# Squares added on VectorE before TensorE sums them over the partitions

## What is computed

```python
def rms_norm(x, g):
    x32 = x.astype(jnp.float32)
    y = x32 * lax.rsqrt(jnp.mean(x32 * x32, axis=-1, keepdims=True) + EPS) * g.astype(jnp.float32)
    return y.astype(x.dtype)

for i in range(DEPTH):                                    # DEPTH = 2
    h = rms_norm(x, ln_mix_g[i])
    x = x + mixer_block(h, ...)      # proj = h @ w_in; q = rms_norm(q_lat, q_norm_g) @ w_uq; kv = rms_norm(kv_lat, ...) @ w_ukv
    h = rms_norm(x, ln_ffn_g[i])
    x = x + hier_moe(h, ...)
    h = rms_norm(x, ln_ple_g[i])
    x = x + jax.nn.sigmoid(h @ w_ple_gate[i]) * (p[i] @ w_ple[i])
return rms_norm(x, final_norm_g)
```

## Time and profile before

| | us |
|---|---|
| median of 3 runs | 1233.9 |
| the runs | 1229.99 to 1234.84 |
| the profiled execution | 1233.92 |
| its span, first to last instruction | 1232.1 |
| TensorE busy | 1135.8 (92%) |
| VectorE busy | 633.6 (51%) |
| ScalarE busy | 355.8 (29%) |
| GpSimd busy | 135.4 (11%) |

### The profile page before, as it was taken

The page is one execution under the profiler, slowest core; times in us unless marked ns, Lnnn a source line. Parts: engine busy times, 40 slices in busy tenths (PEclk is TensorE's granted clock), DMA queues, the critical chain, the costliest instruction groups (busy, mean ns, idle before and its releaser), DMA issues.

```text
span 1232.1 us, 22073 instructions
## 1 busy us (share of the span) xinstructions
PE 1135.8 (92%) x8320; PEld 901.5 (73%) x8320; DVE 633.6 (51%) x1325; ACT 355.8 (29%) x591; POOL 135.4 (11%) x169
## 2 busy tenths in 40 slices
PE   5998889999899999997889979999998999999976
PEld 5987879998765555554879769899986555555576
DVE  4575878655543333334446749775446333333344
ACT  4343443233331111113244344423334111111142
POOL 0110320011000000000102022101101000000001
PEclk9999989999999999998979989999998999999978
DMA  6535876447269999996325369654544999999911
GB/s 173 144 91 151 305 238 186 140 143 216 104 268 418 416 418 418 418 417 195 104 76 155 97 196 344 184 155 137 155 143 176 391 417 418 418 417 418 374 56 65
DMA packets 202708, 300.54 MB, mean 244 GB/s; under 512 B 13969, under 2 KB 166513, under 8 KB 186225
## 3 DMA queue, kind: packets, MB, share of 16 engines
q1 hardware_dynamic: 202608, 299.28, 68.6%
HBM read 298.21 MB, written 1.05 MB: 243 GB/s over the span
## 4 chain that ended last, share of the span: by engine, by line
PE 79%; DVE 8%; DMA 6%; ACT 2%; issue 2%; SPq 2%; POOL 0%; DVEq 0%; POOLq 0%; ACTq 0%
PE ps L688 77%; DMA gu_ring<-in_w_exp_up_dram 4%; PE ps L691 2%; DMA ring<-in_w_in_dram 2%; DVE wsplit L1592 2%; ACT wsplit L1137 1%; SPq L555 1%; SPq L551 1%; DVE work L1696 1%; DVE work L1668 1%; DVE work L1618 0%; DVE h_pair L1601 0%; DVE h_pair L1872 0%; DMA work<-in_x_dram 0%; DVE h_pair L1996 0%
## 5 line engine op out<-in xcount | busy, mean ns | idle before, releaser
L688 PE MATMUL ps<-h_pair,wsplit 128*128 128x256 f32 x3264 | 432.9, 295 | 40.0 <-DVE h_pair L1601 12.2
L688 PEld LDWEIGHTS ps<-h_pair,wsplit 128*128 128x128 f32 x3264 | 418.2, 201 | 50.8 <-issue 33.9
L1592 DVE TENSOR_TENSOR wsplit<-ring,wsplit 128x1024 fp32r<-128x1024 f32 x136 | 168.2, 1239 | 105.8 <-ACT wsplit L1137 95.7
L1137 ACT ACTIVATE wsplit<-ring 128x1024 fp32r<-128x1024 f32 x136 | 141.9, 1056 | 226.5 <-PE ps L688 155.6
L688 PE MATMUL ps<-gu_ring,hT 128*64 128x256 f32 x1280 | 153.7, 383 | 2.4 <-DMA gu_ring<-in_w_exp_up_dram 2.4
L688 PEld LDWEIGHTS ps<-gu_ring,hT 128*64 128x64 f32 x1280 | 88.2, 137 | 65.8 <-issue 20.1
L1696 DVE SCALAR_TENSOR_TENSOR work<-work,convT 128x256 f32<-128x256 f32 x240 | 100.9, 493 | 0.0
L1339 ACT ACTIVATE prow<-ps 128x128 f32<-128x128 f32 x64 | 17.7, 277 | 278.3 <-PE ps L688 278.3
L1959 DVE TENSOR_TENSOR hT_r<-ps,hT_r 128x512 fp32r<-128x512 f32 x64 | 44.3, 692 | 94.0 <-ACT hT_r L1137 94.0
L688 PE MATMUL ps<-work,ring 128*128 128x256 f32 x384 | 88.2, 386 | 0.0
L1945 DVE TENSOR_TENSOR prow<-prow,ps 128x128 f32<-128x128 f32 x64 | 18.4, 288 | 133.8 <-ACT prow L1339 133.8
(11 more groups left out here) (203 smaller groups left out, 1048.7 us busy)
## 6 DMA issues: line engine op xcount, KB each, us to landing
ring<-in_w_in_dram SPq DMA_DIRECT2D x104, 512.0 KB, 4.4
gu_ring<-in_w_exp_gate_dram SPq DMA_DIRECT2D x40, 1024.0 KB, 14.9
gu_ring<-in_w_exp_up_dram SPq DMA_DIRECT2D x40, 1024.0 KB, 17.2
down_ring<-in_w_exp_down_dram SPq DMA_DIRECT2D x40, 1024.0 KB, 19.3
lent_down<-in_w_exp_down_dram SPq DMA_DIRECT2D x24, 1024.0 KB, 19.8
ring<-in_w_exp_gate_dram SPq DMA_DIRECT2D x12, 1024.0 KB, 14.9
ring<-in_w_exp_up_dram SPq DMA_DIRECT2D x12, 1024.0 KB, 17.2
lent_gate_up<-in_w_exp_gate_dram SPq DMA_DIRECT2D x12, 1024.0 KB, 15.7
```

Source lines behind the costliest of these rows:

```text
L688: return nc.tensor.matmul(o, lhsT, rhs, start=first, stop=last)
L1137: return nc.scalar.activation(o, i, ACT.Copy)
L1592: TT(tile_split[:, m, 1, :, :], tile_of(name, m), tile_split[:, m, 0, :, :].bitcast(F32), ALU.subtract).then_inc(tile_low, 1)
```

## The change

VectorE adds the chunks of squares before TensorE sums over the partitions. The new function `add_squares` adds the second, third and fourth pair of chunks to the first pair (128x512 each, in place), and then the second chunk of that pair to the first (128x256). TensorE's `stat` is given that one chunk: 2 matmuls instead of 16 or 12. This is done for x at the start of a layer and at the end of the program, for the queries (two pairs and the halves) and for the embedding. The sums of keys and values and of the layer norm stay as they are. `sq_added` is a new semaphore; each addition waits for ScalarE's pair of squares and for the addition before it, and TensorE's sum waits for the last one.

```diff
+            def add_squares(name, sq, pairs):
+
+                done = SQUARES_ADDED.index(name)
+                for i in range(1, pairs):
+                    dve.wait_ge(sq_ready, after(SQUARES, f"{name}{i}"))
+                    if i > 1:
+                        dve.wait_ge(sq_added, done + i - 1)
+                    TT(sq[:, 0:2, :], sq[:, 0:2, :], sq[:, 2 * i:2 * i + 2, :], ALU.add).then_inc(sq_added, 1)
+                dve.wait_ge(sq_added, done + pairs - 1)
+                TT(sq[:, 0, :], sq[:, 0, :], sq[:, 1, :], ALU.add).then_inc(sq_added, 1)
...
                 project_split("kv", "mix")
-                stat("mix", [sq_x[:, c, :] for c in range(DC)], sq_events("mix", DC))
+                stat("mix", [sq_x[:, 0, :]], [(sq_added, all_added("mix"))])
...
                 project_split("gg0")
-                stat("q", [sq_q[:, c, :] for c in range(6)], sq_events("q", 6))
+                stat("q", [sq_q[:, 0, :]], [(sq_added, all_added("q"))])
...
                 project_split("pg0", "ple")
-                stat("ple", [sq_p[:, c, :] for c in range(DC)], sq_events("ple", DC))
+                stat("ple", [sq_p[:, 0, :]], [(sq_added, all_added("ple"))])
...
             begin(pe, DEPTH + 1)
-            stat("mix", [sq_x[:, c, :] for c in range(DC)], sq_events("mix", DC))
+            stat("mix", [sq_x[:, 0, :]], [(sq_added, all_added("mix"))])
...
                 low_tiles(l, "kv")
 
+                add_squares("mix", sq_x, 4)
                 mean("mix", D)
...
                 evacuates(TT(kr[NOPE:QK, 1, :], bank("rotk")[NOPE:QK, 0:S], sinT[NOPE:QK, :], ALU.mult), "rotk")
+                add_squares("q", sq_q, 3)
                 scale_out("gg0", two(glu_t[0][:, 0, :]))
...
                 low_pair(3)
+                add_squares("ple", sq_p, 4)
                 low_tile(l, "pg1", 0)
...
             begin(dve, DEPTH + 1)
+            add_squares("mix", sq_x, 4)
             mean("mix", D)
```

More of the change, by code:

```diff
@@ L127, with all_added @@
 POWS = ["mix", "kv", "q", "lnv", "ffn", "ple"]
+SQUARES_ADDED = ["mix"] * 4 + ["q"] * 3 + ["ple"] * 4
 SQUARES = ([f"mix{i}" for i in range(4)] + ["kv", "q0", "q1", "q2", "lnv"]
            + [f"ple{i}" for i in range(4)])
+def all_added(name):
+    return len(SQUARES_ADDED) - SQUARES_ADDED[::-1].index(name)
 def after(events, name):
@@ L340, in program @@
         sq_ready = lsem("sq_ready")
+        sq_added = lsem("sq_added")
         tile_high = lsem("tile_high")
@@ L720, in bcast @@
                 last.then_inc(bcast_ready, 1)
-            def sq_events(name, n):
-                return [(sq_ready, after(SQUARES, f"{name}{c // 2}")) for c in range(n)]
             with pe.Fori(0, DEPTH) as l:
```

## The result

| | before | after |
|---|---|---|
| median | 1232.8 (4 runs) | 1220.0 (4 runs) |
| the runs | 1229.99 to 1234.84 | 1217.69 to 1220.91 |
| the profiled execution | 1233.92 | 1220.91 |
| its span | 1232.1 | 1219.1 |

The ratio is 0.9894 with a 95% interval of 0.9869 to 0.9918: the kernel became 12.8 us faster. The forecast was 1207, with a range of 1202 to 1217, so the gain came out at half of what it said: 26.7 us were expected, and 13.0 separate the two profiled executions.

A forecast was written before the change was run, and what follows sets the result against it. The prediction took TensorE to bound the kernel (79% of the span). Matmuls 16.6, clock 9.0 and end 2.7, less 1.6 for a new wait, gave 26.7 us off 1233.9: 1207 us, range 1202 to 1217.

The forecast's parts named there:

- The matmuls removed: Shorter TensorE sums for x, queries and embedding save 3.1, 2.2 and 3.0 us a layer, 16.6 us in two.
- The clock behind the six sums: Behind the sums for x, queries and embedding the clock no longer falls to half: 9.0 us in two layers.
- Rival 1: The clock's falls belong to the stretch, not to the long sums, and stay: 1216 us, 12%.
- The additions: VectorE's additions for x and embedding end before TensorE asks: cost 0; four with handings-on take 2.7 us.
- Rival 3: Additions come late, TensorE waits at all seven sums and restarts at low clock: slower, 1248 us, 3%.
- The new wait: At the spread of the queries' norm TensorE waits 0.8 us for VectorE's diagonal, twice: 1.6 us lost.
- The end: The program's last sum, not hidden and at half clock, gets shorter though it waits for the additions: 2.7 us gained.
- Weights arrive for later stages by semaphores of the stages before: In later stages weight transfers start earlier along with the stages before, so nothing catches up on the gain.
- Rival 2: In the mixer a weight transfer hides the gain of the queries' sum and clock, 3.6 us a layer: 1214 us, 8%.

The follow-up runs named there:

- e10: The changed kernel with TensorE's common branch first and each one-column matmul on the added squares issued 4 times, 8 in a sum: 1212.1 us.
- e11: The changed kernel with TensorE's common branch first and one-column matmuls repeated to sums of 16 and 12, as before the change: 1232.4 us.
- e4: The changed kernel, additions kept, each one-column matmul on the added squares issued 8 times (6 for the queries): 1237.1 us.
- e7: The changed kernel with TensorE's two branches exchanged, so that it tests for the common case first: 1205.6 us.
- e9: The kernel before with TensorE's two branches exchanged, so that it tests for the common case first: 1229.4 us.
- e1: The changed kernel with 100 executed semaphore increments ahead of TensorE's first wait: 1212.0 us.
- e5: The changed kernel with 100 instructions in TensorE's branch for crowded experts, which is never executed: 1210.1 us.
- e2: The kernel before with 156 executed semaphore increments at TensorE's start: 1262.0 us.
- e3: The changed kernel with SyncE's 3 MB for the fifth expert asked for only after the first expert's first product: 1222.0 us.
- e6: The kernel before with 156 instructions in TensorE's branch for crowded experts, which is never executed: 1245.0 us.
- e12: The changed kernel with 200 instructions in TensorE's branch for crowded experts, which is never executed: 1212.2 us.

## Why the prediction was wrong, point by point

- **The matmuls removed, 16.6 us.** Right: 3.20, 2.24 and 3.12 us in layer 0 (forecast 3.1, 2.2, 3.0). The group of one-column matmuls has 108 records, as said.
- **The clock behind the six sums, 9.0 us.** Right in all six places: the key projection takes 3.51 (said: 3.5), gv0 6.0 without its wait (5.9), the first half of pg1 2.94 (3.0). e10 against e11 confirms the cause, and the size (1.6 a fall, against 9.0 / 6 = 1.5) as well as medians that vary by 4 us can. The Trainium skill's rule weighed there, by which a drop comes from an idle gap, doesn't fit these falls: in e4 and e11 they are back with no gap in TensorE's work just ahead of them. Rival 1 fell.
- **The additions, 0 in the layers.** Right. VectorE's timeline of the changed kernel at x, at the queries and at the end:

```profile
22.32 2.28 DVE L1569 TENSOR_TENSOR work<-work 128x512 f32<-128x512 f32 x3
24.64 0.42 DVE L1571 TENSOR_TENSOR work<-work 128x256 f32<-128x256 f32 x1
...
52.25 1.83 DVE L1569 TENSOR_TENSOR work<-work 128x512 f32<-128x512 f32 x2
54.12 0.42 DVE L1571 TENSOR_TENSOR work<-work 128x256 f32<-128x256 f32 x1
...
1207.98 2.28 DVE L1569 TENSOR_TENSOR work<-work 128x512 f32<-128x512 f32 x3 [1.96 <-ACT work L1147]
```

  Those at x end at 25.06, 0.8 us ahead of TensorE's sum, those of the embedding at 585.91 against 588.50. They take the forecast 2.7 us. Rival 3 wanted 1.8 an addition; only the queries' first ones are slowed, the two taking 1.83 beside GpSimd's work.
- **The new wait, 1.6 us.** 0.78 us twice, for `diag L1589`. The mechanism and the range (0.45 to 1.25) were right; that the middle taken in it fits to the tenth is luck.
- **The end, 2.7 us.** Right: the last sum starts 3.97 us behind the first square and is over 0.88 later, 4.85 in all. In the kernel before the transposes follow 7.53 us behind the first square (1217.32 and 1224.85), 2.7 more.
- **"Weights arrive for later stages by semaphores of the stages before, so their transfers start earlier with them and nothing catches up on the gain."** This step failed. The weights did start earlier, by 5.4 us (346.37 to 340.95); TensorE's waits for the experts' weights are not longer (2.3 us in all instead of 2.4). But the sum treated the removed instructions as time only and not as places in the program, and so put what else the change does to the experts' stage at nothing. Those 96 moved the end of a block to 12 instructions behind a branch target, next to a burst of 3 MB, at 6.5 to 7.3 us a layer (some 1.5 of it, in layer 0, may be a low clock that stands there without the stop too). No part of the profile of before shows this stop; only the wait of 1.6 us for "issue" at the branch, with 6 in total, hinted that fetching was on the path here. Rival 2, a transfer that takes part of the gain, was nearest in kind, but put it on the weights' side and in the mixer, and gave it 3.6 a layer.

What remains between the 26.7 forecast and the 23.8 of e7 against e9 is within what these runs vary (e7's own runs span 8 us), and the comparisons don't settle it: e1, with its padding taken off, stands 27.2 us below the kernel before, and e5 21.2.

The trace doesn't say for which engine a packet of q8 is. But all nine stops in these traces (two each in the changed kernel, e2, e3 and e6, one in e12) end 1.2 to 1.5 us behind the end of such a packet, which leaves little doubt that it is TensorE's. **Open** stays what makes the sequencer ask for a block, and when. Open too is why the sum of 12 behind layer 0's gg0 had a low clock behind it in the kernel before and in no other trace with sums of 12: not in e4 and e11, and not in e2, e6 and e9, which leave the change out. So this one fall, some 1.4 us of the 9.0, is not in every execution.

## What to carry to other kernels

An edit that takes instructions out also moves all code behind it: after each change look at the waits for "issue" of the bound engine, and if a product is cut in its midst, shift the code with a few unexecuted instructions before judging the edit. Put the common branch first, so that no jump stands on the path (14 us here for the changed kernel, 4 for the kernel before). Long runs of one-column matmuls cost twice, once themselves and once by the clock behind them; add on an idle engine first, and sum one chunk.

## What the runs showed of the hardware that was not expected

- Where the code lies is worth 1% either way: 156 unexecuted instructions made the kernel before 1.2% slower, 100 made the changed one 0.8% faster (1220.0 to 1210.1).
- A block's end 3 or 4 matmuls behind a taken branch stops TensorE for 1.5 to 1.7 us on free DMA engines and for 3.0 to 4.5 behind 3 MB of weights. The 32 records around such a stop took 5.4 to 7.4 us instead of 3.67.
- A semaphore increment as an instruction of its own costs TensorE about 0.15 us: from 100 of them (e1) to 156 (e2) its first matmul comes 8.55 us later. The 100 delay it by 6.2 us only, since it waits 10 us for x there anyway.
- Sums of 8 one-column matmuls (1.84 us) leave the clock at 1.00, those of 16 (3.6 us) took it to 0.50 in all 24 places inside the layers (four each in six traces), those of 12 (2.6 us) always in layer 1 and once in six in layer 0.
